# All `lo` subtractions of the weight pieces on VectorE in a two-layer transformer block

## The reference, cut to what matters

```python
def reference(x, ...):
    x = first_block(x, ...)    # modulation vectors from c @ w_ada; w_in; 31-tap depthwise
                               # convolution branch; top-64 sparse attention branch; gates; w_o; FFN
    return second_block(x, ...)  # w_in_2; differential attention; 3-tap convolution; w_out_2; FFN

f = (jax.nn.silu(h @ w_gate[l]) * (h @ w_up[l])) @ w_down[l]
```

## Time and profile before

| | |
|---|---|
| median of 3 runs | 2868.42 us (2863.01 to 2868.69) |
| the profiled execution: its time | 2862.82 us |
| the profiled execution: its span | 2861.0 us |
| PE matmul busy | 2649.4 us, 93% |
| DVE busy | 1510.4 us, 53% |
| ACT busy | 1202.6 us, 42% |
| POOL busy | 1283.8 us, 45% |
| moved by DMA | 580.37 MB, mean 203 GB/s |
| TensorE clock granted, mean | 0.967 |
| POOL L2032, `wlo`, 516 | 1280.0 us, mean 2483 ns |
| DVE L1460, `wlo`, 366 | 466.0 us, mean 1273 ns |
| DVE L1455, `acc`, 352 | 484.4 us, mean 1376 ns |
| DVE L1455, `cv`, 240 | 150.9 us, mean 696 ns |

### The profile page before, as it was taken

The page is one execution under the profiler, slowest core; times in us unless marked ns, Lnnn a source line. Parts: engine busy times, 40 slices in busy tenths (PEclk is TensorE's granted clock), DMA queues, the critical chain, the costliest instruction groups (busy, mean ns, idle before and its releaser), DMA issues.

```text
span 2861.0 us, 29460 instructions
## 1 busy us (share of the span) xinstructions
PE 2649.4 (93%) x11812; PEld 2157.3 (75%) x11812; DVE 1510.4 (53%) x1746; ACT 1202.6 (42%) x1574; POOL 1283.8 (45%) x527
## 2 busy tenths in 40 slices
PE   4989887876899899999999999899999999999998
PEld 2867766665778688888888878777878888888886
DVE  5897799999897534354343342454443222222233
ACT  2433433332434544444444445554454444444443
POOL 1656543355567344444444434333434444444443
PEclk8999998888999999999999999999999999999999
DMA  6876655455567456566565555434545555555553
GB/s 256 309 284 250 230 180 178 175 184 199 207 250 292 153 215 220 194 247 243 213 221 197 185 182 186 149 146 162 191 158 196 188 184 204 191 192 190 190 191 133
DMA packets 80712, 580.37 MB, mean 203 GB/s; under 512 B 8980, under 2 KB 8980, under 8 KB 10560
## 3 DMA queue, kind: packets, MB, share of 16 engines
q1 hardware_dynamic: 78480, 564.82, 54.3%
q10 hardware_dynamic: 1440, 9.82, 0.9%
q0 software_dynamic: 656, 3.86, 0.3%
HBM read 574.79 MB, written 3.67 MB: 202 GB/s over the span
## 4 chain that ended last, share of the span: by engine, by line
PE 70%; DVE 13%; ACT 1%; issue 1%; ACTq 0%
PE bank L654 66%; DVE acc L1455 4%; DVE cv L1455 4%; PE bank L618 1%; DVE wlo L1460 1%; DVE SS L1455 1%; DVE X L1455 1%; ACT whi L1009 0%; DVE SS L1856 0%; PE bank L840 0%; PE bank L945 0%; ACT SS L1338 0%; PE bank L803 0%; PE bank L863 0%; DVE X L1569 0%
## 5 line engine op out<-in xcount | busy, mean ns | idle before, releaser
L2032 POOL TENSOR_TENSOR wlo<-raw,whi 128x1024 fp32r<-128x1024 f32 x516 | 1280.0, 2483 | 1560.1 <-ACT whi L1009 1559.3
L1009 ACT ACTIVATE whi<-raw 128x1024 fp32r<-128x1024 f32 x882 | 933.4, 1059 | 1488.0 <-PE bank L654 1375.8
L1460 DVE TENSOR_TENSOR wlo<-raw,whi 128x1024 fp32r<-128x1024 f32 x366 | 466.0, 1273 | 1165.0 <-ACT whi L1009 1164.9
L654 PE MATMUL bank<-whi,HTh 128*128 128x512 f32 x2560 | 718.9, 403 | 15.8 <-DVE X L1558 9.0
L654 PE MATMUL bank<-wlo,HTh 128*128 128x512 f32 x2560 | 696.2, 394 | 36.0 <-DVE wlo L1460 36.0
L654 PE MATMUL bank<-whi,HTl 128*128 128x512 f32 x2560 | 695.6, 394 | 1.0 <-DVE HTl L1799 1.0
L654 PEld LDWEIGHTS bank<-wlo,HTh 128*128 128x128 f32 x2560 | 486.4, 190 | 142.9 <-DVE wlo L1460 39.0
L654 PEld LDWEIGHTS bank<-whi,HTh 128*128 128x128 f32 x2560 | 480.3, 193 | 121.6 <-issue 23.0
L654 PEld LDWEIGHTS bank<-whi,HTl 128*128 128x128 f32 x2560 | 488.6, 191 | 107.3 <-DVE HTl L1799 1.4
L1455 DVE SCALAR_TENSOR_TENSOR acc<-raw,csil,acc 128x512 f32<-128x512 f32 x352 | 484.4, 1376 | 36.9 <-DMA raw<-in_w_ada 26.4
L654 PE MATMUL bank<-whi,ACTh 128*128 128x512 f32 x704 | 191.0, 393 | 0.0
(11 more groups left out here) (223 smaller groups left out, 1331.9 us busy)
## 6 DMA issues: line engine op xcount, KB each, us to landing
raw<-in_w_in SPq DMA_DIRECT2D x128, 1024.0 KB, 4.8
raw<-in_w_ada SPq DMA_DIRECT2D x96, 1024.0 KB, 5.3
raw<-in_w_gate SPq DMA_DIRECT2D x88, 1024.0 KB, 4.8
raw<-in_w_up SPq DMA_DIRECT2D x88, 1024.0 KB, 4.8
raw<-in_w_down SPq DMA_DIRECT2D x88, 1024.0 KB, 4.8
raw<-in_w_o SPq DMA_DIRECT2D x16, 1024.0 KB, 5.3
raw<-in_w_out SPq DMA_DIRECT2D x16, 1024.0 KB, 4.8
raw<-in_w_attn_out SPq DMA_DIRECT2D x8, 1024.0 KB, 4.9
```

Of the source, the lines that this page charges most:

```text
L654: i = e.matmul(bank[2 * ch.st + t][:, :], (xl if ps == 1 else xh)[:, k, tk(t)], (lo if ps == 2 else hi)[:, j * 512:j * 512 + 512], start=c ...
L1009: return e.activation(dst, src, ACT.Copy, scale=scale)
L1460: e.tensor_tensor(lo, src, r32(hi), S_).then_inc(lo_dve, 1)
L2032: e.tensor_tensor(lo, src, r32(hi), ALU.subtract).then_inc(lo_pool, 1)
```

## The change

Every flag of `on_pool` is now False. DVE issues the subtraction of every piece, POOL issues none and keeps its five DMAs and the identity matrix. `lo_at` follows from the flags, so that PE and SP wait for DVE's semaphore.

```diff
-    on_pool = [p % 6 >= 1 if p < M["wo"] + 32 else p % 2 == 1 for p in R(NP)]
+    on_pool = [False for p in R(NP)]
```

## The result

The changed kernel takes 2777.99 us (median of 4 runs, 2775.81 to 2781.06), against 2866.93 for the kernel before over the runs by then (2863.01 to 2868.69). The ratio is 0.9692, with a 95% interval of 0.9676 to 0.9709: 3.1% faster. The profiled execution went from 2862.82 to 2775.81 us, 87.0 less, where 64 were forecast; the time lies inside the range.

What follows compares the result with a forecast made beforehand. DVE was taken to bound 422.6 to 731.8 us and PE everything from 950 us on, with stages between mixed. Gains of 40 + 9 + 7 + 8 = 64 us from 2862.8 gave 2799 us, range 2760 to 2842.

Steps and rivals of the forecast that it cites:

- POOL holds DVE's SBUF readers, not its PSUM readers: Everywhere: DVE instructions with all inputs in SBUF wait out a running POOL subtraction; `acc` unheld costs 0.775 us.
- Gate projections, 40 us: 422.6 to 731.8 us: 103.4 us of holding returns, 62.2 of subtractions are added; 40 us gained, bounds 12 to 49.
- Keys and selection 7: 353.8 to 422.6 us: DVE's returned holding outweighs 14 added subtractions; 7 us gained, between 8 lost and 9 gained.
- output products 8: 731.8 to 842.7 us: DVE's work falls by 11 us; 8 us gained, between 0 and 14.
- `w_o` 0: 842.7 to 950 us: PE is the bound and covers 27 added subtractions; 0, between 5 us either way.
- First stage, 9 us: 60.2 to 353.8 us: DVE's 245.5 us fall by about 9; 9 us gained, between 6 lost and 40 gained.
- 15 more: First stage: estimated us returned by SBUF readers other than `acc`, beside 71.7 us held on `acc`.
- From 950 us on, 0: 950 us to the end: five us of PE cover hide each of 328 added subtractions; 0 us change.
- The lockstep: Rival, chance 0.14: each DVE iteration waits for `hi`, so about half the gain is lost; 2831 us.
- drop out as the bound of the gates: Rival, chance 0.10: DVE stops being the bound altogether and idle parts go as well; 102 us gained, 2761 us.
- The holding: Rival, chance 0.05: something other than POOL holds DVE's long instructions, so added subtractions come on top; 2988 us.
- No difference: Rival, chance 0.03: loads bound the first stage and the attention chain the middle; time stays at 2863 us.

Runs made afterwards that it cites:

- `e7_twice_gates`: Changed kernel with the subtraction of every second piece of the gate projections done twice on DVE; 2815.7 us.
- `e2_late`: Kernel before, with DVE taking the subtractions only from piece 226 on and POOL keeping five in six earlier; 2863.58 us against 2864.31, ratio 0.9996.
- `e3_idle_tt`: Changed kernel with POOL computing an unused product on a tile of its own in the first stage; 2839.87 us.
- `e4_idle_memset`: Changed kernel with POOL filling an unused tile twice in a row in the first stage, reading nothing; 2774.67 us.
- `e8_low_first`: Changed kernel with DVE's subtraction of piece s+2 moved ahead of the `acc` sums in its loop; 2812.72 us.

## Why the prediction was right, and where it was not

- **The bound by stage.** Right: DVE in the gates (`e7_twice_gates`, one for one), PE behind 950 us (`e2_late`, 0.9996).
- **POOL holds DVE's SBUF readers, not its PSUM readers.** Right for the instructions that carry the sum, and shown by `e3_idle_tt` and `e4_idle_memset`; but "a DVE instruction whose inputs all lie in SBUF" was too wide. The selection's one-input `MAX8` and `MATCH_REPLACE8` read SBUF alone and were never held. From the kernel before, with POOL at a subtraction throughout:

```profile
406.40 2.38 POOL L2032 TENSOR_TENSOR wlo<-raw,whi 128x1024 fp32r<-128x1024 f32 x1 [2.59 <-ACT whi L1009]
...
406.52 0.41 DVE L1640 MATCH_REPLACE8 SC<-STT,SC 128x256 f32<-128x256 f32 x1
406.96 0.43 DVE L1638 MAX8 STT<-SC 128x8 f32<-128x256 f32 x1
```

- **DVE's total.** About 1740 us with 350 given back were forecast, and 1761.8 measured. A subtraction's record is 1.22 us on average, so 516 of them are 630 us and 379 came back: 360 from other instructions, 19 from DVE's own 366 subtractions, which had taken 1.27 each. I had used 1.13 for all, and no term counted the own ones.
- **Gate projections, 40 us.** Measured 43.5. Prices of 0.775 and 0.40 us gave 103.4 us back; measured 103.4 (50.6 + 52.8). That the sum is met to the tenth is luck: `acc` gave 3.4 more than forecast and the taps 3.4 less.
- **Keys and selection 7, output products 8, `w_o` 0.** Measured 5.7, 8.5, 0.4. The working of the 7 was wrong in two places. Of the 80 small instructions on the selection's scores that I took as held, the 48 of the search for the largest were not; the 30 two-input ones were (342/479/2522 ns before, 344/416/485 after) and gave 10 us. And 11 subtractions were added in that stretch, not 14.
- **First stage, 9 us: mis-sized.** It measured 28.4. DVE's busy time fell by 15.3 us, not 9: `acc` gave back 76.5 us (164.68 less 88.15), not 71.7, and DVE's own 14 subtractions, which no term counted, some 3.5; the "15 more" for the other SBUF readers was about right. The larger part is the step from DVE's sum to the stage's length: at equal DVE time the stage is 13 us or more shorter without POOL's subtractions, and why is open. My bound for the term, 40, held it. (The `acc` sums of this stage are 120, so 30 of the 94 `ada` units that DVE adds up: a third, and not two thirds as said above.)
- **From 950 us on, 0.** Measured 1.0, with the exchange at the attention chain as described: the scaling that a POOL subtraction held for 2.40 us now follows a subtraction on DVE and takes 0.28. The timeline of the changed kernel at the same place:

```profile
1792.54 1.23 DVE L1460 TENSOR_TENSOR wlo<-raw,whi 128x1024 fp32r<-128x1024 f32 x1
1793.68 0.17 DVE L1851 RECIPROCAL STT<-STT 128x4 f32<-128x4 f32 x1
1793.89 0.21 DVE L1854 TENSOR_SCALAR STT<-STT,LC 128x1 f32<-128x1 f32 x1
...
1794.02 0.28 DVE L1856 TENSOR_SCALAR SS<-SS,STT 128x128 f32<-128x128 f32 x1
```

- **The time.** The forecast of 2799 was 21 us too high, nearly all of it from the first stage; 2778 lies in the range of the terms, 2775 to 2825, because the first stage's bound was wide.
- **Rivals.** The lockstep took next to nothing back in this order, and 35 us in the other (`e8_low_first`). DVE did not drop out as the bound of the gates. The holding did not stay. No difference: the time moved by 3.1%.
- **The rule against the change** (the Trainium skill, Perfetto Trace Analysis, Optimizing Scalar/DVE Operations: offload when DVE is saturated) would by its first half have had the kernel slower; the runs side with its second sentence, that between GpSimd and VectorE it might not help. Here 611 us of work taken off DVE had cost it 360 us of holding; in the gate projections, where DVE is the bound, it cost 103 and saved some 62.

## What to carry to other kernels

Before work goes to GpSimd to relieve VectorE, or after it has gone, look at the minimum, median and maximum of VectorE's own SBUF-to-SBUF instructions: here a maximum some 2 us above the median, while PSUM readers stayed flat, was time that GpSimd's instruction cost, and it was booked as VectorE's busy time. Price such a move both ways, stage by stage: a held instruction lost up to the length of GpSimd's whatever its own (a `MA` of 0.16 us took up to 2.25), and where TensorE was the bound neither way mattered. When a wait comes to an engine's loop, put the work that is ready ahead of it; here the same instructions in the other order gave up 35 of the 89 us between the medians.

## What the runs showed that was not expected

- A GpSimd fill, which reads nothing, held a one-input VectorE instruction (1.13 us for 0.48) and left two-input ones alone (at most 0.755 us).
- Beside running GpSimd subtractions, one-input VectorE instructions that search (`MAX8`, `MATCH_REPLACE8`) kept their 0.28 to 0.43 us.
- DVE at 92% busy beside a PE that is the bound cost PE nothing over 221.6 us.
- The first stage idles DVE for 11 to 14 us more when GpSimd does the subtractions, at equal DVE time. A later release of a piece's `raw` does not explain it; long held stretches might, and no run here has settled it.
- POOL's 328 subtractions of the late stages could be put on either engine without a measurable difference.
